# Moving spilled products and early picks between three scatter tiles, and one tensor for the fourth one-hot buffer

## The reference, cut to what matters

```python
def peer_ffn(xn, wq, keys, u_tab, v_tab):
    ...
        q = (xb @ wq).reshape(C, PEER_HEADS, 2, PEER_DK_HALF)
        s = jnp.einsum('chpd,hpnd->chpn', q, keys).astype(jnp.float32)
        sv, si = lax.top_k(s, K)
        cand = sv[:, :, 0, :, None] + sv[:, :, 1, None, :]
        cidx = si[:, :, 0, :, None] * N_KEYS + si[:, :, 1, None, :]
        top_s, sel = lax.top_k(cand.reshape(C, PEER_HEADS, K * K), K)
        eidx = jnp.take_along_axis(cidx.reshape(C, PEER_HEADS, K * K), sel, axis=-1)
        g = jax.nn.softmax(top_s, axis=-1)
        u = u_tab[eidx]
        act = jax.nn.gelu(jnp.einsum('chkd,cd->chk', u, xb).astype(jnp.float32), approximate=False)
        w = (g * act).astype(xb.dtype)
        return jnp.einsum('chk,chkd->cd', w, v_tab[eidx])
```

## Time and profile before

| | us |
|---|---|
| median of 3 runs | 2039.13 |
| lowest and highest | 2037.79, 2040.08 |
| the profiled execution, its own time | 2039.35 |
| its span in the trace | 2037.4 |
| PE busy | 2006.5 |
| DVE busy | 1466.5 |
| ACT busy | 992.1 |
| POOL busy | 1046.5 |
| mean granted clock of PE, of full speed | 0.998 |

### The profile page before, as it was taken

One profiled execution on the slowest core, in us unless ns is written; L12 is line 12 of the kernel. 1 busy time (PEld: TensorE's weight loads), 2 busy tenths in 40 slices (PEclk: granted clock), 3 DMA queues, 4 the chain that ended last, 5 costly groups with the idle time before them and its releaser, 6 DMA issues.

```text
span 2037.4 us, 31716 instructions
## 1 busy us (share of the span) xinstructions
PE 2006.5 (98%) x11815; PEld 1800.5 (88%) x11815; DVE 1466.5 (72%) x2840; ACT 992.1 (49%) x1825; POOL 1046.5 (51%) x615
## 2 busy tenths in 40 slices
PE   9999999999899999999999999999999999999998
PEld 8746889999899999999999999999877787877787
DVE  6237538979898568889989899987686544067763
ACT  4337434367789843333333333334556642355643
POOL 3213456864445567775776777674335444411242
PEclk9999999999999999999999999999999999999999
DMA  5330225776678899999999999995312223310021
GB/s 207 81 101 12 74 93 159 252 250 229 209 264 283 317 362 378 396 380 375 356 367 371 390 377 402 353 402 212 124 63 93 88 88 104 101 34 32 22 83 63
DMA packets 152855, 435.31 MB, mean 214 GB/s; under 512 B 14464, under 2 KB 62720, under 8 KB 150528
## 3 DMA queue, kind: packets, MB, share of 16 engines
q1 hardware_dynamic: 111232, 282.29, 39.3%
q0 software_dynamic: 41472, 151.01, 19.7%
HBM read 391.28 MB, written 41.97 MB: 213 GB/s over the span
## 4 chain that ended last, share of the span: by engine, by line
PE 90%; DVE 6%; issue 1%; ACT 1%; DMA 1%; SPq 0%; POOL 0%; DVEq 0%; ACTq 0%
PE bank L525 19%; PE bank L527 19%; PE bank L526 19%; PE bank L931 4%; PE bank L933 4%; PE bank L932 4%; PE bank L912 3%; PE bank L1153 2%; PE bank L700 1%; PE wide L1176 1%; PE wide L1164 1%; PE bank L1176 1%; PE bank L794 1%; PE bank L796 1%; PE bank L795 1%
## 5 line engine op out<-in xcount | busy, mean ns | idle before, releaser
L2722 POOL TENSOR_TENSOR wl<-wraw,wh 128x1024 fp32r<-128x1024 f32 x272 | 673.2, 2479 | 702.7 <-ACT wh L1344 700.2
L1344 ACT CAST wh<-wraw 128x1024 fp32r<-128x1024 f32 x360 | 375.6, 1046 | 180.0 <-PE bank L527 150.2
L525 PE MATMUL bank<-WTH,wh 128*128 128x368 f32 x1024 | 337.2, 329 | 3.1 <-issue 3.1
L526 PE MATMUL bank<-WTL,wh 128*128 128x368 f32 x1024 | 336.5, 329 | 0.0
L527 PE MATMUL bank<-WTH,wl 128*128 128x368 f32 x1024 | 336.5, 329 | 0.0
L525 PE MATMUL bank<-AXH,wh 128*128 128x368 f32 (+1 forms) x832 | 300.5, 361 | 1.6 <-ACT wh L1344 1.6
L527 PE MATMUL bank<-AXH,wl 128*128 128x368 f32 (+1 forms) x832 | 296.8, 357 | 0.0
L526 PE MATMUL bank<-AXL,wh 128*128 128x368 f32 (+1 forms) x832 | 296.7, 357 | 0.0
L931 PE MATMUL bank<-AXH,wh 128*128 128x368 f32 x576 | 196.2, 341 | 9.4 <-issue 4.8
L525 PEld LDWEIGHTS bank<-WTH,wh 128*128 128x128 f32 x1024 | 192.3, 188 | 4.9 <-issue 4.9
L526 PEld LDWEIGHTS bank<-WTL,wh 128*128 128x128 f32 x1024 | 192.3, 188 | 0.0
(11 more groups left out here) (556 smaller groups left out, 4027.1 us busy)
## 6 DMA issues: line engine op xcount, KB each, us to landing
wraw<-in_wstream SPq DMA_DIRECT2D x360, 512.0 KB
g_scratch<-gs SPq DMA_DIRECT2D x12, 2048.0 KB, 8.5
gr<-g_scratch SPq DMA_DIRECT2D x15, 1536.0 KB
a_scratch<-tmp SPq DMA_DIRECT2D x72, 184.0 KB
tmp<-a_scratch SPq DMA_DIRECT2D x44, 184.0 KB
sq<-a_scratch SPq DMA_DIRECT2D x28, 184.0 KB
shifted<-hc_scratch SPq DMA_DIRECT2D x12, 270.0 KB, 4.8
fetched<-in_u_rows,diag POOLq DMA_INDIRECT x144
```

Source lines behind the costliest of these rows:

```text
L525: pe.matmul(o, w1, x1, start=n == 0, stop=False)
L526: pe.matmul(o, w1, x2, start=False, stop=False)
L1344: act.copy(wh[n % NSPLIT][:, :], wraw[n % NRAW][:, :]).then_inc(*w_hi.tell(n))
L2722: return pool.tensor_tensor(lo, src, hi.bitcast(F32), ALU.subtract)
```

## The change

Three tables get other numbers, and the fourth buffer gets another tensor. The 42 spilled products of the stage are split over tiles 1, 2 and 3 as 17, 13, 12 (15, 14, 13 before), the 32 picks as 6, 8, 18 (8, 8, 16). `sq0` and `sq1` become two halves of one tensor, so that DVE writes the fourth one-hot buffer with one instruction, as the others.

```diff
--- before.py
+++ after.py
@@ -191,7 +191,8 @@
     st_gg = sb(ctx, "st_gg", [128, 8])
     sps = sb(ctx, "sps", [128, 8, 8])
     tmp = [sb(ctx, f"tmp{i}", [128, T]) for i in range(3)]
-    sq = [sb(ctx, f"sq{i}", [128, T]) for i in range(2)]
+    both_sq = sb(ctx, "sq", [128, 2, T])
+    sq = [both_sq[:, i, :] for i in range(2)]
     tmps = tmp + sq
     diag = sb(ctx, "diag", [128, 5, 128])
     rb = sb(ctx, "rb", [128, T])
@@ -279,7 +280,8 @@
     hots = [(x[:, 0, :, :], x[:, 1, :, :], x[:, :, :, :]) for x in hots]
     hot2 = below_AXL[:, :, 0:128].rearrange("p (a i) c -> p a i c", a=2)
     hots.append((hot2[:, 0, :, :], hot2[:, 1, :, :], hot2))
-    hots.append((*(x[:, 0:512].rearrange("p (i c) -> p i c", i=4) for x in sq), None))
+    hot3 = both_sq[:, :, 0:512].rearrange("p a (i c) -> p a i c", i=4)
+    hots.append((hot3[:, 0, :, :], hot3[:, 1, :, :], hot3))
     gates = ijg[:, 2, :].rearrange("p (h k) -> p h k", h=8)
     B.close()
 
@@ -1312,7 +1314,7 @@
             done = 0
             begin = EXTRA // 8 if tt == 1 else 0
             for n in range(begin, 16):
-                base, count = ((30, 15), (45, 14), (59, 13))[tt - 1]
+                base, count = ((30, 17), (47, 13), (60, 12))[tt - 1]
                 now, whole = n + 1 - begin, 16 - begin
                 if n == 15:
                     if ahead:
@@ -1324,7 +1326,7 @@
                 if ahead:
                     ahead(KT * base + KT * count * now // whole)
                 scatter((tt - 1) * 128 + n * 8)
-                while picks < (10, 18, 26)[tt - 1] + (8, 8, 16)[tt - 1] * now // whole:
+                while picks < (10, 16, 24)[tt - 1] + (6, 8, 18)[tt - 1] * now // whole:
                     pick()
                     picks += 1
                 while done < ROUTE_STEPS * now // (whole - 1):
@@ -2323,20 +2325,14 @@
                 if q > 3 + EXTRA // 4:
                     dve.wait_ge(*scat_mm.at(q - 4))
                 places = ijgT[:, 0:2, 4 * q:4 * q + 4].unsqueeze(3)
-                if q % 4 == 3:
-                    for x in range(2):
-                        dve.tensor_tensor(hots[3][x], iota_psum.unsqueeze(1).to_broadcast([128, 4, 128]),
-                                          places[:, x].to_broadcast([128, 4, 128]),
-                                          ALU.is_equal).then_inc(*hot.tell((q, x), q))
-                else:
-                    if q == 33:
-                        dve.wait_ge(*ld_e.at("all"))
-                        dve.scalar_tensor_tensor(eidx2, shared[:, 0:EXTRA], 128.0, shared[:, EXTRA:2 * EXTRA], ALU.mult,
-                                                 ALU.add).then_inc(*routed.tell((1, "experts")))
-                        dve.tensor_reduce(token_of, ident.rearrange("p (t a) -> p t a", a=SHARED), AX.X,
-                                          ALU.add).then_inc(*routed.tell((1, "token")))
-                    dve.tensor_tensor(hots[q % 4][2], iota_psum.unsqueeze(1).unsqueeze(1).to_broadcast([128, 2, 4, 128]),
-                                      places.to_broadcast([128, 2, 4, 128]), ALU.is_equal).then_inc(*hot.tell(q))
+                if q == 33:
+                    dve.wait_ge(*ld_e.at("all"))
+                    dve.scalar_tensor_tensor(eidx2, shared[:, 0:EXTRA], 128.0, shared[:, EXTRA:2 * EXTRA], ALU.mult,
+                                             ALU.add).then_inc(*routed.tell((1, "experts")))
+                    dve.tensor_reduce(token_of, ident.rearrange("p (t a) -> p t a", a=SHARED), AX.X,
+                                      ALU.add).then_inc(*routed.tell((1, "token")))
+                dve.tensor_tensor(hots[q % 4][2], iota_psum.unsqueeze(1).unsqueeze(1).to_broadcast([128, 2, 4, 128]),
+                                  places.to_broadcast([128, 2, 4, 128]), ALU.is_equal).then_inc(*hot.tell(q))
 
         spilled = [0]
```

## The result

The change made the kernel slower, by 0.16%. The interval, 0.10% to 0.23%, is clear of zero; the difference is smaller than the 0.2% that the forecast had taken as its border.

The account below looks back on a forecast made before the run. PE was taken as the bound, busy 2006.5 of 2037.4 us. With tile 2's end unchanged, -4.0 +0.3 +0.3 gave -3.4 us: 2039.13 to 2035.7 us, ratio 0.9983, range 2031.3 to 2039.3.

Parts of the forecast that it names:

- Tile 1: First tile of 128 tokens: two products more, two picks fewer, ending 1.0 us later, a gain of 7.0 us.
- PE comes 8.6 us later against DVE: At the first wait of tile 1, PE has 6.0 us more work done before it and DVE 2.6 us less.
- So both go: In tile 1, PE's waits of 1.94 and 2.62 us vanish with 1.6 us of slow clock, 6.16 us.
- Rival C: Tile 1's extra products don't fit, ACT waits for the second product in double calls; 2.6 to 4.2 us lost; chance 0.18.
- The rule on the shared interface: Two-input DVE instructions and POOL instructions reading SBUF don't share a read interface; the later waits; applied to tile 3's picks.
- rival D: Tile 3's picks meet POOL each time, giving 2046.5 us; decides once the mean pick exceeds 2.25 us; chance 0.07.
- Tile 2: Second tile: DVE sets the pace, so 4.0 us less PE work shortens it by only 1.0 us; it ends as before.
- 3.0 of the 7.0 us are handed back here: In tile 2, 4.0 us less work shortens the tile by 1.0 us, returning 3.0 us of tile 1's gain.
- Tile 3: Third tile: one product fewer saves PE 4.0 us, less 0.3 us for a stall at the start; gain 3.7 us.
- Behind tile 3: At the fifth U product, PE waits 0.3 us for the last block of gates to be written.
- The fourth buffer: Writing it with one instruction saves DVE 0.06 to 0.07 us, 23 times, some 0.5 us in each tile.
- within 0.2%: Outcome class for the whole kernel: time within 0.2% (4.1 us) of before; chance 0.51.

Follow-up runs that it names:

- undo_merge: The changed kernel with the fourth one-hot buffer written by two instructions again; 2043.86 us, ratio 1.0021 to the kernel before.
- p15_14_13: The changed kernel with the spilled products 15, 14, 13 of the kernel before; 2035.72 us, ratio 0.9976 to the kernel before.
- p16_14_12: The changed kernel with the spilled products split 16, 14, 12; 2035.25 us, ratio 0.9975 to the kernel before.
- cap_call10: The changed kernel with one step moved behind call 10 of tile 1 (96 steps ahead, not 97); 2039.47 us, ratio 0.9995 to the kernel before.
- split_xor: The changed kernel with DVE's xor over 128x2048 written as two instructions of 128x1024; 2041.10 us, ratio 1.0002 to the kernel before.

## Why the prediction was wrong

**Tile 1 is the step that failed.** I had it end 1.0 us later than before; it ended 535.17 - 528.18 = 7.0 us later. The difference of 6.0 us is the new wait, 3.91; some 1.1 us of lower clock behind it (call 10 to call 11 takes 509.67 - 501.77 = 7.90 us, the calls behind 6.79); 0.5 at ijgT, where the wait stayed at 2.69 and the step that I had put into it was not gained; and 0.45 by which the first call stood later in this execution (434.44 against 433.99; in undo_merge it is at 433.94). With the 0.9 us that tile 2 did not give (below) these are the 7.0 us between the forecast end of the stage, 3.7 us earlier than before, and the measured one, 3.3 later.

The words that failed are "PE comes 8.6 us later against DVE" and "So both go". That the old waits go was right; p15_14_13 shows that DVE's 2.8 us alone take them away. The step failed in that it put no wait in their place. I compared PE with DVE only, and by a lead that grows evenly: 12 steps by the first wait. Where the products stand was not looked at call by call. The rule for the steps (8 x 17 x n // 14) and the rule for the products (17 x n // 14) are rounded apart from each other, and at call 10 they ask for a step of a product whose weight tile is cast in the same call. This could have been worked out ahead, from the table of numbers alone and the rows of a cast and a split: two lines of arithmetic for each of the three double calls.

**Rival C came nearest**, with the right calls and a price of 2.6 to 4.2 us against the 5.0 of wait and clock. Its mechanism was another: it had ACT waiting for the second product. What the rows show is PE waiting for the second product's weight tile. Its argument against, ACT busy 71.52 of 100 us, says nothing on an order within a call.

**The rule on the shared interface hit where I did not look.** The trace of the changed kernel shows a split of 4.3 us that began 0.17 us behind an xor of 2.29. The Trainium skill (SBUF — State Buffer, "Who interferes with whom") says that a VectorE instruction with two SBUF inputs contends with a GpSimd instruction that reads SBUF, and that the order in which they start decides who waits. The trace agrees: PE waits 3.91 us here, 2.08 to 2.09 where the xor came after the split, and 2.83 with the xor halved. In the prediction I used it on the picks of tile 3 alone (rival D), with POOL as the one that holds. Here DVE holds POOL, and it is the saving on DVE in tile 1 that brought it there: with eight picks DVE comes to the xor at 498.26 to 499.37, with six at 496.03 to 496.60, just as the split is due. It costs 1.8 us of wait.

**Tile 2 had the right bound, and a length that was 0.9 us off.** It was to be 1.0 us shorter from a later start, so to end where it ended before. It is 0.1 us shorter, 89.60 against 89.69, with 4.0 us less work for PE. Its first call did come 0.5 us sooner behind the last one of tile 1. Of the 4.0 us, 2.3 went into waits: PE waits 2.48 and 1.08 us where it had waited 0.67 and 0.57. The longer one is the profile's "issue" and not POOL's low part as forecast, but DVE's lateness stands ahead of it:

```profile
602.98 2.16 ACT L1598 ACTIVATE hots<-hots,ijgT 128x128 f32<-128x128 f32 x7 [1.55 <-DVE hots L2334]
...
604.12 0.41 PE L933 MATMUL bank<-AXH,wh 128*128 128x368 f32 x1 [2.48 <-issue]
```

The other 1.6 us went into slow clock behind that wait, a term that the forecast for tile 2 did not have. The forecast also tied a gain to this tile: "3.0 of the 7.0 us are handed back here", which holds only where tile 1 takes the products for less than tile 2 gives. Tile 2 gives 0 to 1.6 us for its 14th product, so that product should have stayed there. I had nearly this number, 1.0, and it spoke for p16_14_12 or p15_14_13; both are some 8 us faster than the changed kernel.

**Tile 3 was right in sum**: 78.07 against 81.65, 3.6 shorter where I had 3.7. The stall of 0.3 us that I had put at the start is not there; one of 0.28 is in the middle (657.74). Rival D did not come: the 18 picks take 1.74 us on average, and it needed 2.25. But its rule is in this tile too. In five of the six kernels with 18 picks and 12 products late in the tile a pick began 0 to 0.2 us ahead of a split; the split took 3.3 to 3.5 us in place of 2.4 and PE waited 0.55 to 0.76. In the sixth, cap_call10, the split came first, and tile 3 takes 77.17 like the kernels with 16 picks. So two picks more cost 0.9 us or nothing. The changed kernel, then cap_call10:

```profile
693.50 3.37 POOL L2718 TENSOR_TENSOR wl<-wraw,wh 128x1024 fp32r<-128x1024 f32 x1 [1.10 <-ACT wh L1346]
...
693.38 1.21 DVE L2377 SCALAR_TENSOR_TENSOR fetched<-fetched,below_XH 128x1024 f32<-128x1024 f32 x1
```
```profile
689.53 2.40 POOL L2718 TENSOR_TENSOR wl<-wraw,wh 128x1024 fp32r<-128x1024 f32 x1 [0.40 <-ACT wh L1346]
...
690.12 2.90 DVE L2377 SCALAR_TENSOR_TENSOR fetched<-fetched,below_XH 128x1024 f32<-128x1024 f32 x1
```

**Behind tile 3** PE stands for 58.00 - 57.87 = 0.13 us between 702 and 760, where I had 0.3 for the write. Right.

**The fourth buffer**: 0.06 to 0.07 us on each of 23 instructions was forecast. The merged instruction shows 1.21 us, as the others, and the next one starts 1.13 us behind it, where two instructions take 1.20 in undo_merge. So the saving is there. Nothing of it is seen in the time: undo_merge and the changed kernel have medians of 2043.86 and 2043.33, within the scatter of both.

**The range** ended at 2039.3, just above the middle of rival C. It should have reached C's far end: 2.6 and 1.6 us of clock on top of the forecast, 2039.9, and the rule on the interface in the same calls; even so the measured 2043.33 is beyond it. The chance of "within 0.2%" was the largest, 0.51, and the time is within 0.2%, but on the other side of before: that it came out there is luck, since the 0.51 was given for times below or about that of before.

## What to carry to other kernels

Where two rounded schedules run beside each other (steps and products, loads and uses), compare them entry by entry for every new count: an even spread on average says nothing on the one place where a step falls ahead of its own operand. Before work is moved between stages, ask of each what its last unit costs; in a stage that another engine sets, taking a unit out gains less than the unit (here 0 to 1.6 us of 4.0). And an engine relieved of work comes earlier to all that follows: look what it meets there.

## What the runs showed of the hardware

- A DVE xor over 128x2048 (two inputs in SBUF, 2.28 us) that started 0.09 to 0.17 us ahead of a POOL split of 128x1024 stretched the split from 2.4 to 4.3 and 4.4 us in three kernels. PE waited 1.8 us longer for it than where the xor came behind the split. The other way round, in p16_14_12, the split began 0.33 us earlier and the xor took 4.44:

```profile
494.10 2.62 POOL L2718 TENSOR_TENSOR wl<-wraw,wh 128x1024 fp32r<-128x1024 f32 x1 [3.82 <-ACT wh L1346]
...
494.43 4.44 DVE L2292 TENSOR_TENSOR spare<-selu,sie 128x2048 uint32<-128x2048 uint32 x1
```

- POOL has its turn between two DVE instructions that stand in a row: halving the DVE instruction shortened POOL's hold by 1.1 us.
- After waits of 2.08, 2.09, 2.09 and 2.12 us at the same place the granted clock from 500 to 505 us was 0.78, 1.00, 1.00 and 0.66, and behind one and the same wait for ijgT (2.69 us) 1.00 and 0.66 in two executions of one kernel. After 2.83 us, in split_xor, it was 1.00. Behind the wait of 2.5 us in tile 2 a lower clock cost 1.6 us in five executions and nothing in two. What decides it stays open; the runs here don't tell.
